# Scores and values with one 448-column product for the high weight parts, values in two passes over the experts

## What is computed

```python
def block(args):
    xb, eb, gb = args
    ue = jnp.take(expert_u, eb, axis=0)
    act = jax.nn.gelu(jnp.einsum('nhkd,nd->nhk', ue, xb), approximate=False) * gb
    return jnp.einsum('nhk,nhkd->nd', act, jnp.take(expert_v, eb, axis=0))
...
x = x + peer(h2, ...)
return rms_norm(x, final_norm_w)
```

## Time and profile before

| | us |
|---|---|
| median of three runs | 2376.08 |
| lowest and highest | 2372.18, 2376.28 |
| the profiled execution | 2374.39 |
| its span, first to last instruction | 2372.6 |
| TensorE busy | 2338.8 |
| VectorE, ScalarE, GpSimd busy | 1526.2, 1340.8, 830.7 |

### The profile page before, as it was taken

How to read it: one execution, slowest core, us unless ns; L and a number is a source line. 1 busy time by engine, 2 the same in 40 slices (tenths; PEclk the granted TensorE clock), 3 DMA queues, 4 the chain that set the end, 5 groups by cost and what they waited for, 6 DMA issues and landing times.

```text
span 2372.6 us, 51129 instructions
## 1 busy us (share of the span) xinstructions
PE 2338.8 (99%) x19066; PEld 2203.6 (93%) x19066; DVE 1526.2 (64%) x2468; ACT 1340.8 (57%) x2369; POOL 830.7 (35%) x612
## 2 busy tenths in 40 slices
PE   9999999999999999999999999999999999999998
PEld 8888787978888789999999999999999999999998
DVE  5568988557566565675667877776456566666534
ACT  5456554255544545777776666666555555555555
POOL 0000201100000002445556545554556566666554
PEclk9999999999999999999999999999999999999999
DMA  7665554046666557666778766675777777777684
GB/s 215 186 195 151 160 168 152 22 128 193 194 195 215 169 182 230 193 199 220 240 260 283 255 216 233 227 242 165 259 252 248 266 248 256 260 256 262 226 256 147
DMA packets 197218, 499.52 MB, mean 211 GB/s; under 512 B 14726, under 2 KB 82824, under 8 KB 187656
## 3 DMA queue, kind: packets, MB, share of 16 engines
q1 hardware_dynamic: 187719, 430.20, 57.1%
q0 software_dynamic: 9408, 68.16, 8.2%
HBM read 491.98 MB, written 5.24 MB: 210 GB/s over the span
## 4 chain that ended last, share of the span: by engine, by line
PE 92%; DVE 3%; ACT 2%; DMA 1%; POOL 1%; issue 1%; SPq 0%; ACTq 0%
PE PS L920 19%; PE PS L923 10%; PE PS L518 9%; PE PS L867 9%; PE PS L868 9%; PE PS L871 9%; PE PS L561 5%; PE PS L563 5%; PE PS L562 5%; PE PS L520 4%; PE PS L511 3%; PE PS L879 2%; DVE w_lo L1437 1%; POOL big L1364 1%; DMA raw<-in_w_out 0%
## 5 line engine op out<-in xcount | busy, mean ns | idle before, releaser
L958 ACT ACTIVATE w_hi<-raw 128x512 fp32r<-128x512 f32 x1576 | 985.6, 631 | 919.9 <-PE PS L923 291.3
L1437 DVE TENSOR_TENSOR w_lo<-raw,w_hi 128x512 fp32r<-128x512 f32 x1064 | 748.3, 715 | 759.1 <-ACT w_hi L958 757.1
L1392 POOL TENSOR_TENSOR w_lo<-raw,w_hi 128x512 fp32r<-128x512 f32 x512 | 707.7, 1392 | 1095.4 <-ACT w_hi L958 1089.3
L920 PE MATMUL PS<-act_both,w_hi 128*128 128x224 f32 x4096 | 540.5, 274 | 0.0
L920 PEld LDWEIGHTS PS<-act_both,w_hi 128*128 128x128 f32 x4096 | 498.5, 192 | 0.2 <-DVE act_both L2083 0.2
L867 PE MATMUL PS<-act_both,w_hi 128*128 128x224 f32 x2048 | 489.0, 277 | 3.6 <-ACT big L1239 3.6
L868 PE MATMUL PS<-act_both,w_hi 128*128 128x224 f32 x2048 | 483.2, 274 | 0.0
L867 PEld LDWEIGHTS PS<-act_both,w_hi 128*128 128x128 f32 x2048 | 393.0, 192 | 4.3 <-issue 4.3
L868 PEld LDWEIGHTS PS<-act_both,w_hi 128*128 128x128 f32 x2048 | 393.1, 192 | 0.0
L518 PE MATMUL PS<-act_both,w_hi 128*128 128x512 f32 x1056 | 373.2, 400 | 6.9 <-DVE w_lo L1437 6.1
L923 PE MATMUL PS<-act_both,w_lo 128*128 128x224 f32 x2048 | 312.1, 275 | 0.3 <-POOL w_lo L1392 0.2
(11 more groups left out here) (261 smaller groups left out, 1930.6 us busy)
## 6 DMA issues: line engine op xcount, KB each, us to landing
raw<-in_peer_u_t SPq DMA_DIRECT2D x256, 512.0 KB, 4.3
raw<-in_peer_v SPq DMA_DIRECT2D x256, 512.0 KB, 4.7
raw<-in_w_in SPq DMA_DIRECT2D x180, 512.0 KB, 3.8
raw<-in_w_out SPq DMA_DIRECT2D x32, 512.0 KB, 4.5
raw<-in_peer_w_q SPq DMA_DIRECT2D x32, 512.0 KB, 4.3
raw<-in_w_ret_branch SPq DMA_DIRECT2D x16, 512.0 KB, 4.4
raw<-in_w_rwkv_branch SPq DMA_DIRECT2D x16, 512.0 KB, 4.5
big<-in_x SPq DMA_DIRECT2D x2, 1024.0 KB, 5.9
```

Of the source, the lines that this page charges most:

```text
L920: pe.matmul(v_bank(j), w_hi[:, k % 2, cols], act2[:, b, w, :], start=first and j % 2 == 0 and w == 0, stop=False)
L958: act.activation(w_hi[:, slot % 2, hh * 512:(hh + 1) * 512], raw[:, slot, hh * 512:(hh + 1) * 512], ACT.Copy).then_inc(S["unit_hi"], 1)
L1392: pool.tensor_tensor(w_lo[:, k % 2, cols], raw[:, k, cols], w_hi[:, k % 2, cols].bitcast(f32), ALU.subtract).then_inc(S["p_split"], 1)
L1437: dve.tensor_tensor(w_lo[:, slot % 2, cols], raw[:, slot, cols], w_hi[:, slot % 2, cols].bitcast(f32), ALU.subtract).then_inc(S[done], 1)
```

## The change

1. In scores and values the two matmuls with the high weights become one of 448 columns, whose moving operand is the high and the low part of the activation side by side. Its result takes 448 columns of a bank: two halves that have to be added.
2. In scores VectorE adds them (`usum`) and writes to SBUF; ScalarE then does gelu in place. `usum` stands at the start of a gate turn's half, and before that behind the work of every even unit.
3. In values a result tile now fills a bank, so only eight fit. The stage goes in two passes `h` over all 128 blocks, each for 1024 channels; a unit is one block's half, and `act2` has four slots, filled once for each unit.
4. Each pass ends in `last_units`: the last two units go tile by tile. After pass 0 VectorE sums the even tiles, ScalarE copies the odd ones and GpSimd sums those; after pass 1 VectorE sums all eight, TensorE turns all sixteen tiles, and the additions follow.
5. The turned rows start at token 32, so tokens 0 to 31 are the last rows of the second tile; loads of `x1` and stores have a piece more. `MAC_AT`, `ADD_AT` and `FINAL_AT` move.

```diff
-MAC_AT = [66 + 8 * t // 5 for t in range(PICK_TILES)]
+MAC_AT = [66 + 8 * t // 5 for t in range(17)] + [100 + 5 * t // 4 for t in range(PICK_TILES - 17)]
-IDS_AT, ADD_AT, FINAL_AT = 15, 118, 54
+IDS_AT, ADD_AT, FINAL_AT = 15, 119, 24
...
             def um(it, k):
-                        wait_past(pe, S[f"gelu{k // 2}"], it)
+                        wait_past(pe, S[f"gelu{k // 2}"], 2 * it - 1)
...
-                        pe.matmul(out, w_hi[:, k % 2, cols], act_hi[:, kc, SPARSE:TOK], start=kc == 0, stop=False)
-                        pe.matmul(out, w_hi[:, k % 2, cols], act_lo[:, kc, SPARSE:TOK], start=False, stop=False)
+                        pe.matmul(pair_bank(bank), w_hi[:, k % 2, cols], act_both[:, kc, :, SPARSE:TOK], start=kc == 0, stop=False)
...
+            def vm(h, it, k, first=False):
+                pe.wait_ge(S["act2_split"], it * 4 + (h * BLOCKS + k + 1))
...
-                        for w in range(2):
-                            pe.matmul(v_bank(j), w_hi[:, k % 2, cols], act2[:, b, w, :], start=first and j % 2 == 0 and w == 0, stop=False)
+                        if first:
+                            bank_free(h, j)
+                        pe.matmul(pair_bank(j), w_hi[:, k % 2, cols], act2[:, k], start=first, stop=False)
...
+            def last_units(h):
+                it = BLOCKS // 4 - 1
+                for j in range(8):
+                    cols, halves = slice(j * P, (j + 1) * P), j // 4 + 1
+                    for k in (2, 3):
...
+                        pe.matmul(pair_bank(j), w_hi[:, k % 2, cols], act2[:, k], start=False, stop=False)
+                    for k in (2, 3):
...
+                        last = pe.matmul(PS[:, j, 0:DT], w_lo[:, k % 2, cols], act2[:, k, 0, :], start=False, stop=k == 3)
...
+                    last.then_inc(S["tile_done"], 1)
+                    if h == 1 and j in (2, 4, 6):
+                        turn_rows((j - 2) // 2)
+                if h == 1:
+                    turn_rows(3)
...
             def late_gelu(i, b):
-                act.wait_ge(S["half_used"], i * 8 + (2 * U0 + 8 * GATE_AT + 4 * b + 4))
...
-                act.activation(late_out[b], PS[:, 4 + b, 0:DT], ACT.Gelu).then_inc(S[f"gelu{b}"], 1)
+                act.wait_ge(S[f"gelu{b}"], 2 * i + (2 * GATE_AT + 1))
+                act.activation(late_out[b], late_out[b], ACT.Gelu).then_inc(S[f"gelu{b}"], 1)
...
+            def usum(it, b, late=True):
+                dve.wait_ge(S["half_used"], it * 8 + (2 * U0 + 4 * b + 4))
+                dve.tensor_reduce(late_out[b] if late else G[:, 2 * it + b, :], summed(4 + b), AX.X, ALU.add).then_inc(S[f"gelu{b}"], 1)
...
             def gate_turn(i):
                 for par in range(2):
+                    usum(i + (GATE_AT - 1), par, not first)
                     if not first:
                         gate_in(i - 1, par)
...
             def u_step(unit):
...
+                if unit >= 4 and k % 2 == 0:
+                    usum(it - 1, k // 2, False)
...
+            def sum_tile(h, j):
+                dve.wait_ge(S["tile_done"], 8 * h + j + 1)
+                dve.tensor_reduce(out_T[h][:, j, :], summed(j), AX.X, ALU.add).then_inc(S["out_even"], 1)
...
-            for q in range(4):
-                even_out(2 * q)
-                if q > 0:
-                    add_last(0, q - 1)
-                    add_last(1, q - 1)
-            add_last(0, 3)
-            add_last(1, 3)
+            for j in range(8):
+                sum_tile(1, j)
+                if j in (4, 6):
+                    for tt in range(2):
+                        add_last(tt, (j - 4) // 2)
+            for q in (2, 3):
+                for tt in range(2):
+                    add_last(tt, q)
```

More of the change, by code:

```diff
@@ L921, in vm @@
-                    pe.wait_ge(*split_done("v", it, k, hh + 1))
-                    for j, cols in tiles:
-                        last = pe.matmul(v_bank(j), w_lo[:, k % 2, cols], act2[:, b, 0, :], start=False, stop=final and j % 2 == 1)
-                        if final and j % 2:
-                            last.then_inc(S["tile_done"], 1)
-                    if not final:
-                        last.then_inc(S["half_used"], 1)
-                    elif 2 * (k % 2) + hh > 0:
-                        turn_rows(2 * (k % 2) + hh - 1)
@@ L931, in turn_rows @@
-            def turn_rows(q):
-                pe.wait_ge(S["out_even"], q + 1)
-                pe.wait_ge(S["out_odd"], q + 1)
-                for tt in range(2):
+                        if first:
+                            bank_free(h, j)
+                        pe.matmul(pair_bank(j), w_hi[:, k % 2, cols], act2[:, k], start=first, stop=False)
+                    pe.wait_ge(*split_done("v", it + h * (BLOCKS // 4), k, hh + 1))
+                    for j, cols in tiles:
+                        last = pe.matmul(PS[:, j, 0:DT], w_lo[:, k % 2, cols], act2[:, k, 0, :], start=False, stop=False)
@@ L950, in _, with v_blocks @@
+            for h in range(2):
+                def v_blocks(it, first=False, final=False):
+                    for k in range(2 if final else 4):
+                        vm(h, it, k, first and k == 0)
+                    if final:
+                        last_units(h)
+                v_blocks(0, first=True)
+                with pe.Fori(1, BLOCKS // 4 - 1) as it:
+                    v_blocks(it)
+                v_blocks(BLOCKS // 4 - 1, final=True)
         @block.scalar
@@ L2076, in _ @@
                 gate_turn(i)
[L2077 to L2089 removed]
+            usum(BLOCKS // 2 - 1, 0)
@@ L2096, in v_lo @@
-                    if it == BLOCKS // 2 - 4 and b == 0:
-                        dve.memset(out_T[:, :, 0:SPARSE], 0.0)
+                    if k % 2:
+                        sparse_step(g, k // 2)
             dve.wait_ge(*split_done("u", UPAIRS - 1, 3, 2))
-            for it in range(BLOCKS // 2):
-                v_lo(it)
-            def even_out(bank):
-                dve.wait_ge(S["tile_done"], bank + 1)
-                dve.tensor_copy(out_T[:, 2 * bank:2 * bank + 2, SPARSE:TOK], v_both(bank)).then_inc(S["out_even"], 1)
+            for h in range(2):
+                for it in range(BLOCKS // 4):
+                    v_lo(h, it)
```

220 lines of the change are left out of this document (129 added, 91 removed).

## The result

The changed kernel takes 2394.85 us (median of four runs, 2391.47 to 2396.36); the kernel before, on the same chip, 2375.16 (2372.18 to 2376.28). The ratio is 1.0085, 95% interval 1.0073 to 1.0098: it is slower by 0.85%, where 3% faster was forecast. The profiled execution has a span of 2391.7 us against 2372.6.

What follows compares the result with a forecast made beforehand. TensorE was taken as the bound, with a floor of about 112 ns a matmul. Saving 95.0 - 12 - 6 - 1 - 1.5 - 1 - 1.6 = 71.9 us gave 2304.2 us, range 2280 to 2338.

Steps and rivals of the forecast that it cites:

- merge, 4096 pairs: Scores and values: one matmul of 448 columns at 200.0 ns replaces two of 111.6, saving 23.2 ns a pair, 95.0 us.
- loop before the gates: Scores before the gates: ScalarE and VectorE wait for each other through the sums; 12 us lost, ends 0 and 21.
- loop in the gate turns: Gate turns: gelu waits for VectorE's sum, VectorE for w_hi; 6.25 us half a turn, 6 us lost.
- values with seams: Values: 1 us for weights; seams 1.5 us from scores to values and 1 us at the change of pass.
- end: Last two units: last add ends 11.5 us after they begin, before 10.3; 1.6 us lost (0.5 to 3).
- The formula that I weighed in the prediction: Matmul spacing as N / 2.4 + 2.5 ns; by it the merge would save 10 us, not 95.
- Rivals D and F: D: 448 columns cost what 512 do, 2390 us, chance 0.05. F: distance by columns alone, nothing saved, 2380, 0.03.
- Carrying lateness over: Gate turns: 4 us lost if lateness is carried from turn to turn, 15 if not; 6 taken.
- Rival C: Loops or transfers cost more: 15 us in gates, 21 before, 8 late rows, 8 seams; 2333 us, chance 0.21.
- seams: Stage changes: scores to values 1.5 us (0 to 3), change of pass 1 us (0.3 to 2.5).
- Rival E: Values: VectorE becomes the bound through the port shared with GpSimd, 12.0 us for 10.71 an iteration; 2434 us, chance 0.04.
- my own two signs for being wrong outright: Prediction wrong outright if 448 columns take over 215 ns, or if gate turns stay at 12.5 us.

Runs made afterwards that it cites:

- b_values_small_pool: Changed kernel with GpSimd making the low part of only 64 of its 512 columns of each pair in values; 2380.36 us, ratio 1.0024.

## Why the prediction was wrong

The sum against what was measured, in spans. The merge's gain is what TensorE's own pace from start to start gives: an iteration of scores 10.76 us before and 10.13 after, half a gate turn 6.25 and 5.96, half a unit of values 1.340 and 1.260. That is 22.4 us before the gates, 16.5 in them and 40.9 in values and end, 19.5 ns a pair. A stage's loss is its time less that of before, and this gain on top.

```
                                   predicted      measured
merge, 4096 pairs                    +95.0         +79.8
loop before the gates                -12           -17.4
loop in the gate turns                -6           -61.0
values with seams                     -3.5         -18.9
end                                   -1.6          -3.3
start                                  0            +1.7
together                             +71.9         -19.1
```

- *The merged product.* 448 columns cost 202.7 ns, forecast 200.0 (ends 197.4 and 225.6), but the term came out 15 us short. Two things took them. The window counts of the earlier trace rows have some two matmuls too many: from start to start the trace of before has 226.7 ns for 512 columns, and 125.7 for 256 with them, which would have given 201.4 for 448. And in place, beside 224 columns, four pairs take 1.260 to 1.267 us, 315 to 317 ns a pair, where I had 311.6. An early iteration of scores takes 10.13 us, forecast 9.97. The formula that I weighed in the prediction, which the Trainium skill ("TensorE: Matmul & The Clock Gate", "Back-to-back issue gap") gives for an isolated matmul, makes 448 columns 189.2 ns and two of 224 191.7; the traces have 202.7 and 223.3 and disagree for this type. For a stream of weight loads and matmuls the same section gives about 81 ns at 128 columns and 131 at 512; the trace of before has 112 and 226.7. Rivals D and F are out.
- *The step that failed: the loop in the gates*, 6.25 us for half a turn, measured 7.40. It was the right loop with one wrong term, 2.98 us from w_hi to the end of the low pair, measured 4.15. (The 48 matmuls and 8 records of the earlier trace rows that the prediction calls a gate turn are half of one; its 12.5 us are right.) I took VectorE's half low part at 0.61, from the row at 1341.42 in the earlier trace rows. It stands in the gap between two pairs of GpSimd's, whose rows in the trace of before are these:

```profile
1337.44 2.80 POOL L1392 TENSOR_TENSOR w_lo<-raw,w_hi 128x512 fp32r<-128x512 f32 x2 [3.45 <-ACT w_hi L958]
...
1343.70 2.80 POOL L1392 TENSOR_TENSOR w_lo<-raw,w_hi 128x512 fp32r<-128x512 f32 x2 [2.08 <-ACT w_hi L958]
```

  The earlier trace rows had what such work costs beside it: 0.96 and 1.48. What I had not seen is that the loop brings the two together: ScalarE, held up in gelu, does its next four w_hi in a row, and both subtracters start at once. Of the 55 intervals between gate products 32 take 7.4 us and the others 6.3 to 7.0; together they are 388.7 - 55 x 5.96 = 61 us over TensorE's pace. With the forecast's 6 us there in place of 61 the change would have gained some 36 us instead of losing 19.
- *Carrying lateness over* (0.15 x 28 rather than 0.74 x 20) was a choice between two small numbers, and it doesn't matter once every half with a sparse step is over TensorE's pace. Rival C's worst case for the gates was 15 us.
- *Before the gates.* The sum of 10.7 to 10.9 us for an iteration of the last six was 12.1 on average in the trace; the one step read above, a sparse step at 2.3 in place of 1.2 us, again beside GpSimd, is most of the difference there. The six are 11.6 us over TensorE's 10.13, where I took 5. Iterations 18 to 28 are 9.4 us over it, where I took 9, but 5.4 of them are in one iteration (1172.8 to 1188.3), not spread as I had them.
- *Values.* I let a subtraction cost 0.92, the mean of before. Done twice as often, and in each iteration beside GpSimd, it costs 1.06, and lo and sparse steps are stretched too: VectorE 9.0 of 10.13 us in the stretch without waits, not 8.2. That ScalarE waits for nothing of VectorE's here held, but single steps of 4 us come often enough. GpSimd's share is worth 14.5 us by b_values_small_pool in time, 18.4 by its stage, of a loss of 18.9. The changed kernel's stage is 19.8 us over 508 halves of 1.260: some 12.4 in the six waits, 2.3 in halves of 1.267, and 5.1 at the seams (forecast 2.5). In b_values_small_pool the seams are 1.4 and the rest is gone. Rival E, the port as the bound in values, was right in kind at a fifth of its price, and I had excluded it from scores by its wording.
- *The end.* The last add ends 12.3 us after the last two units begin (forecast 11.5, before 10.3):

```profile
2368.99 0.59 PE L961 MATMUL PS<-act_both,w_hi 128*128 128x448 f32 x2
...
2378.28 0.62 DVE L2142 TENSOR_REDUCE big<-PS 128x224 f32<-128x448 f32 x1
2378.82 2.47 DVE L2179 TENSOR_TENSOR big<-big,PS 128x512 f32<-128x512 f32 x4
...
2378.96 0.84 PEld L948 LDWEIGHTS PS<-cst,big 128*128 128x128 f32 x8 [0.90 <-DVE big L2142]
```

TensorE's last turn of results waits 0.9 us for the last sum, which I had counted beside TensorE's work.

Of my own two signs for being wrong outright, 448 columns over 215 ns did not come; turns that stay at 12.5 us was the right place: they went to 14.3 us on average (400.1 / 28) from 12.7.

## What to carry to other kernels

When a change makes engine A wait for B where B already waits for A, write the loop out, and price each member as it will run *in step with* the others, not as it ran in a trace where they were spread out: an engine that was held up does its queue in one burst, and those that lengthen one another meet there. Here the cure was not less work but one place in the order: put the instruction that waits (gelu) behind the work on which its own answer depends (w_hi), and leave it a unit of slack.

## What the hardware showed that I had not expected

- VectorE and GpSimd subtracting from SBUF at the same time lengthen one another, by up to the whole of the other's work: a pair of 512 columns takes VectorE 1.29 us with GpSimd nearly idle and 2.38 to 4.87 beside it; 224 columns 0.38 and 1.44 (two in 2.89 us at 1901.70 of the changed kernel); a sparse step 1.28 and 3.96. The sum, which reads PSUM, takes 0.63 us at most in the 44 cases of the changed kernel that lie within a GpSimd subtraction, and 0.61 away from them. The Trainium skill ("SBUF — State Buffer", "SBUF: two separate sides") describes an exclusive lock held for a whole instruction, with the loser fully blocked. The traces agree: two subtractions of 224 columns take about as long as GpSimd's two of 512, and the sparse step at 1801.78 gained 2.7 us, the length of a whole pair of GpSimd's. The record of that step starts 0.32 us ahead of GpSimd's pair (1802.10, 2.55 us), while GpSimd still issues a gather, and it is the step that gets longer: the starts in a profile don't tell who will wait.

```profile
1901.70 2.89 DVE L2151 TENSOR_TENSOR act_both<-big,act_both 128x224 fp32r<-128x224 f32 x2
...
1901.21 3.14 POOL L1438 TENSOR_TENSOR w_lo<-raw,w_hi 128x512 fp32r<-128x512 f32 x2 [2.50 <-ACT w_hi L994]
```

- Widths of 448 and 224 columns mix at next to no cost (1.260 us for four pairs, 1.257 by the widths alone), and an operand of two pieces of 224 with a gap is at most 1% dearer than one piece: gate turns of scores with it reach 5.96 us a half, by 16 x 0.3144 + 8 x 0.112 = 5.93.
- Why the values stage of kernels with the same code there takes 651.7 to 661.0 us is not settled: the waits are the same in kind, and their number differs; the halves of 1.267 in place of 1.260 us make 2.3 us at most. No run was made on it.
